# A hybrid decoder step on one core: a new order in the embedding stage, and experts with six split weight pieces

## What the kernel computes

```python
hp = layer_norm(concatenate([meta, x_prompt]), ln_emb_g, ln_emb_b)      # embedding
hs = layer_norm(x_sample, ln_emb_g, ln_emb_b)
... = split(h @ w_in, idx, axis=-1)                                      # 16 low-rank columns, q, k, ...
scores = scores + rel_bias_for(dist, rel_bias)                           # table[bucket] per head
...
expert = grp * EXPERTS_PER_GROUP + top_i                                 # router
buf = zeros((n_blocks * 128, 1024)).at[dest].set(x[tok_s])               # tokens sorted by expert
hb = silu(xb @ w_gate[e]) * (xb @ w_up[e])                               # one block of 128 tokens
out = hb @ w_down[e]                                                     # 1024x512, 1024x512, 512x1024
h2 = layer_norm(ALPHA * h1 + segment_sum(out[dest] * w_s), ln2_g, ln2_b)
```

## Time and profile before

| | |
|---|---|
| Median of 3 runs | 1961.63 us (1961.19 to 1962.73) |
| Profiled execution | 1960.17 us, its span 1958.6 us |
| Busy, share of the span | PE 1756.3 us (90%), DVE 1158.8 (59%), ACT 815.7 (42%), POOL 317.0 (16%) |

### The profile page before, as it was taken

One profiled execution on the slowest core, in us unless ns is written; L12 is line 12 of the kernel. 1 busy time (PEld: TensorE's weight loads), 2 busy tenths in 40 slices (PEclk: granted clock), 3 DMA queues, 4 the chain that ended last, 5 costly groups with the idle time before them and its releaser, 6 DMA issues.

```text
span 1958.6 us, 28511 instructions
## 1 busy us (share of the span) xinstructions
PE 1756.3 (90%) x8894; PEld 1438.7 (73%) x8894; DVE 1158.8 (59%) x1669; ACT 815.7 (42%) x1444; POOL 317.0 (16%) x390
## 2 busy tenths in 40 slices
PE   2899999899999999999977997179999999999965
PEld 2899999688788788878746886067777777777742
DVE  5411110577777768867762332947777777777717
ACT  2332221344345435434311222136666666666623
POOL 1200000122322322232100111310000000000025
PEclk9999999899999999999966998579999999999978
DMA  6487521434423433333379225549999999999954
GB/s 208 144 256 204 171 70 50 140 100 144 143 91 115 159 123 104 120 105 101 98 240 319 75 106 198 189 162 381 399 399 397 399 399 397 399 400 397 348 200 187
DMA packets 240657, 422.91 MB, mean 216 GB/s; under 512 B 24976, under 2 KB 123168, under 8 KB 240344
## 3 DMA queue, kind: packets, MB, share of 16 engines
q1 hardware_dynamic: 187120, 321.93, 46.2%
q0 software_dynamic: 20048, 69.06, 10.1%
q10 hardware_dynamic: 33408, 30.94, 4.5%
HBM read 354.83 MB, written 78.55 MB: 221 GB/s over the span
## 4 chain that ended last, share of the span: by engine, by line
PE 35%; issue 7%; DVE 5%; DMA 1%; POOL 1%; ACT 1%; POOLq 0%; DVEq 0%; SPq 0%; ACTq 0%
PE PS L1922 8%; PE PS L1924 8%; PE PS L1923 8%; PE PS L2233 6%; PE PS L1929 2%; PE PS L2089 1%; PE PS L2096 1%; POOL hh L967 1%; PE PS L2119 1%; DVE zz L1894 1%; DVE ya L1906 0%; DMA yc<-obuf_dram,ridx 0%; PE PS L2201 0%; PE PS L2129 0%; DVE st L557 0%
## 5 line engine op out<-in xcount | busy, mean ns | idle before, releaser
L1789 DVE TENSOR_TENSOR wm_lo<-raw,wm_hi 128x2048 fp32r<-128x2048 f32 x156 | 352.0, 2289 | 147.8 <-ACT wm_hi L1299 147.7
L1299 ACT CAST wm_hi<-raw 128x2048 fp32r<-128x2048 f32 x160 | 301.6, 1907 | 75.7 <-PE PS L1924 75.7
L1922 PE MATMUL PS<-w_hi,hT_hl 128*128 128x512 f32 (+1 forms) x584 | 233.5, 400 | 13.8 <-DMA hT_hl<-hl_dram 9.1
L1923 PE MATMUL PS<-w_lo,hT_hl 128*128 128x512 f32 (+1 forms) x584 | 227.5, 390 | 0.0
L1924 PE MATMUL PS<-w_hi,hT_hl 128*128 128x512 f32 (+1 forms) x584 | 227.1, 389 | 0.0
L1922 PE MATMUL PS<-wm_hi,xT_hi 128*128 128x512 f32 x512 | 204.0, 398 | 3.1 <-DVE xT_lo L1854 3.1
L1924 PE MATMUL PS<-wm_hi,xT_lo 128*128 128x512 f32 x512 | 201.2, 393 | 0.0
L1923 PE MATMUL PS<-wm_lo,xT_hi 128*128 128x512 f32 x512 | 200.9, 392 | 0.0
L1962 PE MATMUL PS<-xa_hi,wn 128*128 128x384 f32 x480 | 162.8, 339 | 0.2 <-ACT ev L1074 0.2
L1964 PE MATMUL PS<-xa_hi,wn 128*128 128x384 f32 x480 | 162.2, 338 | 0.0
L1963 PE MATMUL PS<-xa_lo,wn 128*128 128x384 f32 x480 | 162.2, 338 | 0.0
(11 more groups left out here) (345 smaller groups left out, 3332.9 us busy)
## 6 DMA issues: line engine op xcount, KB each, us to landing
raw<-in_w_gate SPq DMA_DIRECT2D x64, 1024.0 KB, 8.7
raw<-in_w_up SPq DMA_DIRECT2D x64, 1024.0 KB, 10.0
raw<-in_w_down SPq DMA_DIRECT2D x64, 1024.0 KB, 10.2
hT_hl<-hl_dram POOLq DMA_DIRECT2D x70, 512.0 KB, 5.2
braw<-in_w_in SPq DMA_DIRECT2D x16, 1024.0 KB, 6.3
obuf_dram<-yb ACTq DMA_DIRECT2D x32, 512.0 KB, 6.9
nd_dram<-ev ACTq DMA_DIRECT2D x72, 192.0 KB, 2.7
nd<-nd_dram SPq DMA_DIRECT2D x36, 384.0 KB, 3.7
```

The costliest lines, as they stand in the source:

```text
L1299: act.copy(wm_hi[:, j], raw[:, j]).then_inc(m_hi[j // 4], 1)
L1789: dve.tensor_tensor(wm_lo[:, j], raw[:, j], BF(wm_hi[:, j]), ALU.subtract).then_inc(m_lo[j // 4], 1)
L1922: pe.matmul(out, x_hi, w_hi_, start=start, stop=False)
L1923: pe.matmul(out, x_hi, w_lo_, start=False, stop=False)
```

## The change

**Embedding.** The position rows (clears, table, PE's products, copies) move behind the sixth block on DVE; on PE they come in four parts after the fourth and fifth units and the first two gate products of round one, all through bank 2. SP loads the table later and stores `brow` after the last block's rows. POOL makes its constants before the semaphore credits (12 of them first); ACT waits for three constants in place of six and normalizes blocks 0 and 1 before it casts a weight chunk. DVE's order becomes: statistics and mean term of a block with a chunk's low part between them (`e_norm`), then scaling and low parts. SP puts three chunks and the third block ahead.

**Experts.** All six pieces are split, with six raw buffers; the second raw buffer of piece 5 and `hT_f` go. Partition p holds weight rows 8p to 8p+7 (4p to 4p+3 for the down weights), so a piece is 8 KB contiguous per partition; the tokens and hidden values are transposed with a stride to match (`strided_transposes`). ACT copies the whole result, and DVE's `y_half` goes. `h1l` keeps six blocks in place of eight; three are loaded late.

```diff
@@ SP
-        sp.dma_start(relb[:], A["rel_bias"]).then_inc(c_rin, 16)
-        sp.dma_start(onehot[:], A["onehot"]).then_inc(c_rin, 16)
...
-        raw_load(0)
+        raw_load(0)
+        raw_load(1)
+        x_load(2)
+        raw_load(2)
...
+        sp.dma_start(relb[:], A["rel_bias"]).then_inc(c_rin, 16)
+        sp.dma_start(onehot[:], A["onehot"]).then_inc(c_rin, 16)
...
-        sp.wait_ge(c_rel, 7)
-        sp.dma_start(brow_dram.rearrange("h (p j) -> p h j", p=P), brow[:]).then_inc(c_brow, 16)
         h_store(0)
         x_load(3)
-        raw_load(4)
+        raw_load(3)
...
+        for b in range(3, 9):
+            h_store(b)
+            if b + 3 < NB:
+                x_load(b + 3)
+        sp.wait_ge(c_rel, 7)
+        sp.dma_start(brow_dram.rearrange("h (p j) -> p h j", p=P), brow[:]).then_inc(c_brow, 16)
...
-            v = src[ds(e, 1)].rearrange("o (k p) n -> p (o k) n", p=P)
+            v = src[ds(e, 1)].rearrange("o (p k) n -> p (o k) n", p=P)
...
-        def m_down(t, s):
+        def m_down(t):
...
-            sp.wait_ge(*piece_lo(t - 1, 4))
-            m_load(e, 4, 4, w_raw[4])
-            sp.wait_ge(*piece_used(t - 2, 5))
-            m_load(e, 5, 5 + s, m_raw[s])
+            for j in (4, 5):
+                sp.wait_ge(*piece_lo(t - 1, j))
+                m_load(t, e, j)
@@ POOL
-        for s in step_sems:
-            pool.sem_inc(s, CREDIT)
         pool.memset(ones[:], 1.0).then_inc(c_id, 1)
...
+        for s in step_sems[:EARLY]:
+            pool.sem_inc(s, CREDIT)
         pool.wait_ge(c_id, 3)
...
+        for s in step_sems[EARLY:]:
+            pool.sem_inc(s, CREDIT)
@@ ACT
-        act.wait_ge(c_id, 6)
+        act.wait_ge(c_id, 3)
...
         first(0, 0)
+        first(1, 1)
         high(0)
+        e_hT(0)
         high(1)
-        first(1, 1)
-        e_hT(0)
-        high(2)
         first(2, 0)
         e_hT(1)
+        high(2)
+        e_hT(2)
+        first(3, 1)
         high(3)
-        first(3, 1)
-        e_hT(2)
...
-        for j in range(5):
+        for j in range(6):
             high(0, j)
...
                 high(t, 4)
+                high(t, 5)
             act.wait_ge(u_T, upto(NB + t))
-            act.copy(hT_f[:], PS[:, 4, 2 * P:])
-            act.copy(hT_hi[:], PS[:, 4, 0:2 * P]).then_inc(u_c, 1)
+            act.copy(hT_hi[:], PS[:, 4]).then_inc(u_c, 1)
...
-            act.copy(yb[s][:, 0:512], PS[:, 5]).then_inc(m_ya, 1)
+            act.copy(yb[s][:], PS[:, 5:7].rearrange("p a n -> p (a n)")).then_inc(m_ya, 1)
@@ DVE
+        def e_norm(b, between=None):
+            e_stats(b, b % 2)
+            if between is not None:
+                low(between)
+            e_mean(b, b % 2)
+
+        e_norm(0)
+        e_norm(1)
+        dve.wait_ge(c_in, 32)
+        e_scale(0, 0)
+        e_scale(1, 1)
+        low(0)
+        e_low(0)
+        e_norm(2, 1)
+        e_scale(2, 0)
+        e_low(1)
+        e_norm(3, 2)
+        e_low(2)
+        e_scale(3, 1)
+        low(3)
+        e_norm(4, 4)
+        e_scale(4, 0)
+        low(5)
+        e_low(3)
+        e_norm(5)
+        e_scale(5, 1)
+        e_low(4)
+        e_norm(6)
+        e_scale(6, 0)
+        e_low(5)
+
         dve.memset(brow[:, :, 0:WIN], NEG)
...
+                            PS[:, 2].rearrange("p (h n) -> p h n", h=4)).then_inc(c_rel, 1)
+
+        e_norm(7)
+        e_scale(7, 1)
         e_low(6)
+        e_norm(8)
         e_scale(8, 0)
...
+                low(t, 5)
             dve.wait_ge(u_c, upto(NB + t))
-            dve.tensor_tensor(hT_lo[:], PS[:, 4, 0:2 * P], BF(hT_hi[:]), ALU.subtract).then_inc(m_hlo, 1)
-            if prev:
-                y_half(t - 1, 1 - s, uses)
+            dve.tensor_tensor(hT_lo[:], PS[:, 4], BF(hT_hi[:]), ALU.subtract).then_inc(m_hlo, 1)
@@ PE
+        def position_rows(a):
+            pe.wait_ge(c_rel, 3 + a)
+            for h in range(4):
+                last = pe.matmul(PS[:, 2, h * P:(h + 1) * P], relw[:, 4 * a + h, :], onehot[:], start=True, stop=True)
+            last.then_inc(c_rpe, 1)
...
+                elif tc == 0:
+                    position_rows(c - 3)
             for g in range(G):
                 project("gk", g, 5, tc)
+                if tc == 0 and g < 2:
+                    position_rows(2 + g)
...
+        def strided_transposes(bank, src, count):
+            parts = src[:].rearrange("p (n k) -> p k n", k=count)
+            for k in range(count):
+                last = pe.transpose(PS[:, bank + k // 4, (k % 4) * P:(k % 4 + 1) * P], parts[:, k], ident[:])
+            return last
...
-            for k in range(2):
+            for k in range(DE // P):
+                j = 4 + k // 2
...
-                    last = pe.matmul(PS[:, 5 + half], hT_f[:, k * P:(k + 1) * P], raw[:, 5 + s, c:c + 512],
-                                     start=False, stop=(k == 1))
```

More of the change, by code:

```diff
@@ L55 @@
 CREDIT = 4
+EARLY = 12
 IN_Q, IN_K, IN_V, IN_R, IN_LR, IN_QA, IN_KA, IN_VA, IN_GA, IN_GB = (
@@ L595, in _ @@
             sp.dma_start(prime_dram[i], prime[:]).then_inc(s, 16)
[L597 to L602, removed]
-        sp.wait_ge(c_rel, 7)
-        sp.dma_start(brow_dram.rearrange("h (p j) -> p h j", p=P), brow[:]).then_inc(c_brow, 16)
         h_store(0)
         x_load(3)
-        raw_load(4)
+        raw_load(3)
         h_store(1)
         x_load(4)
+        raw_load(4)
+        h_store(2)
+        x_load(5)
         raw_load(5)
-        for b in range(2, 7):
+        for b in range(3, 9):
             h_store(b)
@@ L815, in _ @@
         sp.wait_ge(o_lg, upto(8))
-        for b in range(NB - 1):
+        for b in range(NB - 3):
             f_load(b)
@@ L862, in _ @@
         sp.dma_start(ln2_b[:], A["ln2_b"][0:1, :].to_broadcast([P, D])).then_inc(f_small, 16)
-        f_load(NB - 1)
+        for b in range(NB - 3, NB):
+            f_load(b)
         for b in range(NB):
@@ L1011, in _ @@
         last = 2 * iters + 1
-        pool.wait_ge(m_yd, upto(last))
+        pool.wait_ge(m_ya, upto(last))
         wait_apart(pool, m_yo[0], 16 * (iters + 2))
@@ L1932, in _ @@
         pe.wait_ge(c_id, 6)
-        pe.wait_ge(c_rel, 3)
-        for a in range(4):
+        def position_rows(a):
+            pe.wait_ge(c_rel, 3 + a)
             for h in range(4):
-                last = pe.matmul(PS[:, 4 + a, h * P:(h + 1) * P], relw[:, 4 * a + h, :], onehot[:], start=True, stop=True)
+                last = pe.matmul(PS[:, 2, h * P:(h + 1) * P], relw[:, 4 * a + h, :], onehot[:], start=True, stop=True)
             last.then_inc(c_rpe, 1)
-        pe.wait_ge(c_rel, 7)
         def e_transposes(b):
@@ L2216, in up, with down @@
                     last.then_inc(m_used[j // 4], 1)
[L2218 removed]
+        def down(t):
             pe.wait_ge(m_hlo, upto(t))
             pe.wait_ge(m_ya, upto(t - 1))
[L2221 to L2223 removed]
+            for k in range(DE // P):
+                j = 4 + k // 2
+                if k % 2 == 0:
+                    pe.wait_ge(*piece_lo(t, j))
                 for half in range(2):
[L2225 removed]
+                    c = (k % 2) * D + half * 512
                     last = split_product(PS[:, 5 + half], hT_hi[:, k * P:(k + 1) * P], hT_lo[:, k * P:(k + 1) * P],
[L2227 to L2235 removed]
+                                         wm_hi[:, j, c:c + 512], wm_lo[:, j, c:c + 512], k == 0, k == DE // P - 1)
+                if k % 2 == 1:
+                    last.then_inc(m_used[j // 4], 1)
         def x_transposes(t, s, uses):
@@ L2239, in x_transposes, with m_step @@
             pe.wait_ge(t_lo, upto(NB + t - 1))
-            transposes(0, xw[s], KC).then_inc(t_T, 1)
-        def m_step(t, s, uses, before, prev, more):
+            strided_transposes(0, xw[s], KC).then_inc(t_T, 1)
+        def m_step(t, s, uses, prev, more):
             pe.wait_ge(t_lo, upto(NB + t))
@@ L2251, in m_step @@
             if prev:
-                down(t - 1, 1 - s, before)
+                down(t - 1)
             pe.wait_ge(m_hm, upto(t))
             pe.wait_ge(m_hlo, upto(t - 1))
-            transposes(4, hm, DE // P).then_inc(u_T, 1)
+            strided_transposes(4, hm, DE // P).then_inc(u_T, 1)
         x_transposes(0, 0, 0)
-        m_step(0, 0, 0, None, False, True)
+        m_step(0, 0, 0, False, True)
         with pe.Fori(0, iters) as i:
-            m_step(2 * i + 1, 1, i + 1, i, True, True)
-            m_step(2 * i + 2, 0, i + 1, i, True, True)
-        m_step(2 * iters + 1, 1, None, iters, True, False)
-        down(2 * iters + 1, 1, iters)
+            m_step(2 * i + 1, 1, i + 1, True, True)
+            m_step(2 * i + 2, 0, i + 1, True, True)
+        m_step(2 * iters + 1, 1, None, True, False)
+        down(2 * iters + 1)
         pe.wait_ge(m_ya, upto(2 * iters + 1))
-        pe.wait_ge(m_yd, upto(2 * iters + 1))
         for b in range(NB):
```

103 lines of the change are left out of this document (34 added, 69 removed).

## The result

The change makes the kernel faster: 1946.34 us, the median of 6 runs (1942.36 to 1950.48), against 1960.42 us for the kernel before (6 runs, 1954.66 to 1962.73); the ratio is 0.9931, with a 95% interval of 0.9913 to 0.9948. Forecast were 1936 us and a range of 1925 to 1958: right in direction and range, but 14.1 us came where 25.6 had been forecast. The spans of the two profiled executions, 1958.6 and 1945.4 us, differ by 13.2, and two landmarks split them: the first and the last group of token transposes, once per expert block.

What follows compares the result with a forecast made beforehand. TensorE was taken to set the expert stage's pace, with the DMA only just able to follow. 1960.17 - 22.4 (experts) - 3.3 (embedding) + 0.5 (end) = 1935.0 us, with the median 1.5 higher: 1936, range 1925 to 1958.

Steps and rivals of the forecast that it cites:

- TensorE's 17.71 us for a block: Expert stage: 12 split matmuls (2.73 us) replace 8 full-precision passes (3.43 us), 0.70 us saved from 18.41 us a block.
- The DMA's 17.5 us with long runs: Expert stage: weights in 8 KB runs at the store queue's rate need 17.5 us a block, just under TensorE's.
- DVE's cover of 1.9 us: Expert stage: of DVE's 4.5 us of waits a block, 1.9 us remain after its added work and the shorter block.
- Strided weight loads: Rival in the expert stage: strided loads take twice 0.1 us, 1.2 us more a block, 1974 us; 15%, partial price 10%.
- Run length buys nothing: Rival in the expert stage: DMA stays at 18.46 us a block, TensorE gains only some 4 us, 1955 us; 9%.
- a further step as large: Expert DMA's fast end: 8 KB runs gain again as much as from 2 to 4 KB, about 17.1 us a block.
- First projection: Embedding: TensorE's first projection comes near 34 us, 23 us earlier than 56.97, most of it given back later.
- the clock's price: Embedding: TensorE is slow at first after each of two waits, up to 2.3 us each, leaving 3.3 us gained.
- the store of the bias (3 MB) now stands before the chunks of the second head group: Embedding, SP queue: the chunks are needed 30 us later, which covers the store's 10 us.
- Two more 512 KB reloads run beside the first gathers: End of the kernel: the last sums use these reloads some 40 us later; no cost was put down.
- ACT now copies the last result alone, about 0.5 us more: End of the kernel: ACT's lone copy of the last result adds about 0.5 us, the end's only cost.
- its slower end: Upper end of the range, 1958 us: takes in a partial price of the stride and the slow DMA.

Runs made afterwards that it cites:

- run 3: The whole change, but weights in the old order (runs of 2 and 4 KB) and transposes without a stride: 1960.65 us, ratio 1.0011 to the kernel before.
- run 4: The kernel before with only the new weight order and strided transposes, five split pieces and one plain: 1960.26 us, ratio 1.0007.
- run 5: The whole change, but the bias store 11 loads and 18 stores later on SP: 1953.49 us, ratio 0.9967 to the kernel before.
- run 9: The whole change with position rows made early, between the second and third block's transposes, bias store where the change has it: 1926.55 us, ratio 0.9840.
- run 6: The whole change, but position rows made between the second and third block's transposes, bias store after round two's first unit: 1924.53 us, ratio 0.9810.
- run 7: The whole change, but last block's sixth piece cast and subtracted after the hidden values, three reloads after the fourth gathers: 1940.73 us, ratio 0.9891.
- run 10: The whole change with early position rows, mended end (late reloads, late sixth piece) and last block's result copy before the sixth cast: 1914.10 us, ratio 0.9775.
- run 2: The expert part of the change alone, embedding as in the kernel before: 1942.94 us, ratio 0.9922 to the kernel before.

## Why the prediction was right, and where it was off

**Expert stage: right, step by step.** TensorE's 17.71 us for a block is what run 3 shows before its loads fall behind, and the stride adds 0.04. The DMA's 17.5 us with long runs rested on an estimate of 2.48 us a MB; 2.45 was measured, and run 3 shows the 18.46 for short runs (18.43). What the DMA alone would need with long runs is not shown, only that it follows at 17.75. DVE's cover of 1.9 us is 1.8. Strided weight loads, the dearest rival, cost 0.04 to 0.06 us a block in place of 1.2. "Run length buys nothing" falls by run 3 (0.9931 against 1.0011); as that rival had it, TensorE gained until the landing had grown to some 13 us, though 7.3 us in place of its 4. With it falls the rule of 512 bytes that the Trainium skill gives ("DMA: Bandwidth & Descriptors", Specifications), for this queue: 2.62 us a MB with runs of 2 and 4 KB, 2.45 with 8 KB, and the difference decided the block. In the loop 0.66 us a block came where 0.70 had been put down: 1.2 us in 29 blocks, the price of the stride.

The packets of the traces, sorted by size (1700 to 1800 us on the weight queue), say which step of the run length counts: 2.69 us a MB in 2 KB packets (gate, up) and 2.47 in 4 KB packets (down) before, 2.44 in 8 KB packets after and 2.53 in run 4. So it is the step from 2 to 4 KB; the one from 4 to 8 KB adds little or nothing. The other end that the prediction gave its DMA term, "a further step as large", is not there; nor does its "about 17.1 us" follow from its own rates, by which a step of 0.14 us a MB more gives about 16.7. The forecast's 17.5 was the rate of 4 KB rows, so by these figures runs of 4 KB for all pieces might have done as well; that was not run.

**Embedding: the walk was right, the cover was not.** First projection 32.4 (34 forecast), pauses of 6.05 and 4.68 us (5.3 and 4.9). With the clock's price, two times 2.3 us, the forecast was to be 3.3 us ahead, and at the start of the second round 3.8 are there; once that round's low-rank product is copied by ACT, still 1.15 are measured (93.45 against 94.59), so the clock took 2.1 more than was put down for it. The step that failed is the next one: "the store of the bias (3 MB) now stands before the chunks of the second head group; they are needed 30 us later, which covers its 10 us". The chunks were covered. The store runs beside ACT's small stores, which it was not asked about. They land late, ACT's three buffers are full when the gate products come in a burst, and TensorE waits and loses its clock: 4.3 us by runs 5 and 9. From 1.15 us ahead to 4.41 behind are 5.6; the other 1.3 are open. At 171.91 us ACT is 5.45 us later than in the kernel before, and 3.35 of that reach the experts; where the 2.1 between were made good was not looked into. The store was moved three times: out of the burst's way the pause is gone (runs 5 and 6), before the burst of round two it stands there (run 9).

**The end: two covers that were not there.** "Two more 512 KB reloads run beside the first gathers; the last sums use them some 40 us later" named the reloads' own user and not the gathers that they run beside: 2.4 us, and run 7 takes 3.7 off. And "ACT now copies the last result alone, about 0.5 us more" missed that in the last block the sixth piece stands ahead of the hidden values on ACT and DVE with nothing on TensorE to hide it: 2.2 us more of waiting, 2.7 less in run 10.

So three covers failed in the same way: each named who needs the moved transfer or piece, and not who shares a queue or an engine with it. Of the 25.2 us of the sum, 6.65 were lost in the embedding, 1.2 in the loop and 4.1 at the end; 13.2 are left. That the time lies in the range is in part luck: its slower end was for a partial price of the stride and a slow DMA, neither of which came true, and for what was lost it had no term.

## What to carry to other kernels

A large transfer is hidden only if nobody who runs beside it is waited for: look at every small store or gather in its window, not just at its own user. Before it is moved, look for the program's own waits for it as well (run 5). Two edits may each leave the time as it is and together take 15 us off (run 2), where two resources are full at once; test the pair and both halves. Work that must be done once goes where the bounding engine waits anyhow: the position rows took TensorE 7.2 us in its wait (run 6) and 5.5 us between the products (2.07, 1.15, 1.15 and 1.18), and with the waits, the clock and the store about them 21 us lay between the two.

## What the runs showed of the hardware

Reading 128 values 32 or 16 bytes apart does make TensorE's weight load longer, in the groups of the whole change from 1360 to 1850 us:

```profile
L2220 PEld LDWEIGHTS PS<-ident,xw 128*128 128x128 f32 x216 | 28.0, 189 | 2.1
L2220 PEld LDWEIGHTS PS<-ident,hm 128*128 128x128 f32 x112 | 18.0, 206 | 2.1
```

Without a stride both are 140 to 141 ns (run 3), so 48 and 65 ns are added. They stay hidden beside the product before, and the block grows by 0.04 to 0.06 us for 12 of them. This is the Trainium skill's rule of two hits on a 16-byte line ("Advanced Engine Details and Errata", Memory Cachelines) as far as these loads show it: the load is slower, the time is not. DMA reads with 8 KB runs took 2.45 us a MB of 16 engines' time at a DMA share of 1.01, those with 2 and 4 KB 2.62 at 1.04; by packet size, 2.69 for 2 KB, 2.47 for 4 KB and 2.44 for 8 KB (2.53 in run 4). Beside a 3 MB store of SP's queue, a 192 KB store of ACT's queue landed 8.0 us after its issue, against 5.7 at the same place without it. After a wait of 6.05 us TensorE's granted clock was 0.50, its lower level of 1.2 GHz, over 65 to 70 us, and after one of 4.68 us over 85 to 90. The sample attention, which no kernel here changes, took 58.2 us at a mean clock of 0.73 in the whole change and 61.6 at 0.69 in run 6: 3.4 us that no edit in that stage made, and whose cause was not tried.
